# A decoder layer step on one core: weight loads, state rows and a weight split moved, and the causal term of the first head's blocks 2 to 4 added on VectorE

## What is computed

```python
proj = jnp.einsum('btd,dp->btp', xn, w_in)
gb, gc, hc, zc, q, k, v, o, zm, ig, fg = jnp.split(proj, ...)
yc, conv_new = short_conv(gc * hc, conv_buf, conv_w)      # 3 taps
y_conv = gb * yc * jax.nn.silu(zc)
# mLSTM, per head and chunk of 128 tokens
log_d = jnp.where(causal, b[:, None] - b[None, :] + ig[None, :], -jnp.inf)
m_t = jnp.maximum(b + m_prev, jnp.max(log_d, axis=-1))
d = jnp.exp(log_d - m_t[..., None]); inter = jnp.exp(b + m_prev - m_t)
s = (q @ k.T) * d
num = s @ v + inter[..., None] * (q @ c_prev)
den = s.sum(-1) + inter * (q @ n_prev)
h = num / jnp.maximum(jnp.abs(den), jnp.exp(-m_t))[..., None]
c_new = decay * c_prev + einsum(w_last, k, v)             # and n_new, m_new
y_m = rmsnorm_head(h) * gain * sigmoid(o) * silu(zm)
out = x + concat([y_conv, y_m]) @ w_out, then a last rmsnorm
```

## Time and profile before

| what | us |
|---|---|
| median of 3 runs | 1112.46 (1112.3 to 1112.65) |
| the profiled execution | 1110.13 |
| its span, first to last instruction | 1108.3 |
| PE busy, of the span | 1062.8 (96%) |
| DVE busy | 540.1 (49%) |
| ACT busy | 340.1 (31%) |
| POOL busy | 256.0 (23%) |

### The profile page before, as it was taken

How to read it: one execution, slowest core, us unless ns; L and a number is a source line. 1 busy time by engine, 2 the same in 40 slices (tenths; PEclk the granted TensorE clock), 3 DMA queues, 4 the chain that set the end, 5 groups by cost and what they waited for, 6 DMA issues and landing times. The chain is left out here.

```text
span 1108.3 us, 17992 instructions
## 1 busy us (share of the span) xinstructions
PE 1062.8 (96%) x7186; PEld 602.2 (54%) x7186; DVE 540.1 (49%) x1005; ACT 340.1 (31%) x672; POOL 256.0 (23%) x333
## 2 busy tenths in 40 slices
PE   3899999999999999999999999999999999999995
PEld 3555546565666555546665555566655555444442
DVE  5786664557553434575534344755332323433333
ACT  6546434242412232434122323341122131111111
POOL 5002303021212223212122232111211121542422
PEclk9999999999999999999999999999999999999998
DMA  9474532033200211442003114410212062265651
GB/s 248 141 159 85 135 81 49 24 105 101 89 20 19 90 49 57 119 120 89 20 18 91 49 57 138 119 32 20 94 38 90 25 218 92 102 216 209 237 200 77
DMA packets 124184, 108.74 MB, mean 98 GB/s; under 512 B 42384, under 2 KB 109092, under 8 KB 124100
## 3 DMA queue, kind: packets, MB, share of 16 engines
q1 hardware_dynamic: 81952, 65.68, 20.7%
q0 software_dynamic: 7600, 25.03, 6.2%
q10 hardware_dynamic: 34548, 16.87, 5.7%
HBM read 65.43 MB, written 33.41 MB: 89 GB/s over the span
## 5 line engine op out<-in xcount | busy, mean ns | idle before, releaser
L799 PE MATMUL bank<-xTh,Wh 128*128 128x512 f16 (+2 forms) x1304 | 421.5, 342 | 8.1 <-DVE Wl L163 4.9
L800 PE MATMUL bank<-xTl,Wh 128*128 128x512 f16 (+2 forms) x1304 | 424.4, 342 | 0.0
L801 PE MATMUL bank<-xTh,Wl 128*128 128x512 f16 (+2 forms) x1304 | 424.0, 342 | 0.0
L801 PEld LDWEIGHTS bank<-xTh,Wl 128*128 128x128 f16 x1304 | 129.2, 99 | 120.5 <-issue 0.7
L799 PEld LDWEIGHTS bank<-xTh,Wh 128*128 128x128 f16 x1304 | 129.1, 99 | 116.4 <-DVE Wl L163 5.1
L800 PEld LDWEIGHTS bank<-xTl,Wh 128*128 128x128 f16 x1304 | 129.2, 99 | 108.9 <-issue 2.6
L808 PE MATMUL bank<-Wh,xTh 128*128 128x128 f16 x544 | 92.8, 219 | 0.6 <-DVE ysum L163 0.6
L809 PE MATMUL bank<-Wl,xTh 128*128 128x128 f16 x544 | 92.8, 219 | 0.0
L810 PE MATMUL bank<-Wh,xTl 128*128 128x128 f16 x544 | 92.8, 219 | 0.0
L163 ACT ACTIVATE tz<-bank 128x512 f32<-128x512 f32 x32 | 19.1, 597 | 145.1 <-PE bank L801 144.4
L671 POOL TENSOR_TENSOR ysumst<-ysum,ysumst 128x1024 f16<-128x1024 f32 x16 | 34.1, 2128 | 103.6 <-ACT ysumst L163 103.6
(11 more groups left out here) (336 smaller groups left out, 1518.7 us busy)
## 6 DMA issues: line engine op xcount, KB each, us to landing
wst<-in_w_in ACTq DMA_DIRECT2D x29, 512.0 KB, 3.8
xs<-in_x_prompt SPq DMA_DIRECT2D x22, 512.0 KB, 4.2
y_ops<-ysumst POOLq DMA_DIRECT2D x16, 512.0 KB, 3.2
w_ops<-xs SPq DMA_DIRECT2D x16, 448.0 KB, 3.8
out<-xs POOLq DMA_DIRECT2D x11, 512.0 KB, 2.9
Wh<-y_ops SPq DMA_DIRECT2D x12, 448.0 KB, 3.6
Wl<-y_ops SPq DMA_DIRECT2D x12, 448.0 KB, 4.3
y_ops<-yst POOLq DMA_DIRECT2D x16, 256.0 KB, 3.3
```

Source lines behind the costliest of these rows:

```text
L799: mm(out, wh[:, k, :], xh, start=(k == 0), stop=False)
L800: mm(out, wh[:, k, :], xl, start=False, stop=False)
L801: last = mm(out, wl[:, k, :], xh, start=False, stop=(k == KT - 1))
```

## The change

- The three weight loads at the start of block 4 of a head are issued by ACT for the second head only; for the third and fourth head SP issues each one behind the store of the slab that had its buffer (order of buffers 1, 2, 0). ACT's wait for `wo_low` is gone. The states' load stays on ACT.
- The state rows are turned by PE in the middle of the first tile, K of block 0, instead of V's, and copied by DVE behind the first gate scan, ahead of the second weight's Wl.
- The fourth weight of the first head is split in the middle of Q instead of behind V, on ACT and on DVE.
- In blocks n = 1, 2, 3 the exponents go the other heads' way: PE makes A alone, DVE adds the mask, ACT takes `eh` from A first and then `dp`. Block n = 0 stays.

```diff
-SPLIT_AT_HALF = {Q: (4,), GC: (5,), HC: (6,), GB: (7,), ZC: (8,)}
+SPLIT_AT_HALF = {Q: (3, 4), GC: (5,), HC: (6,), GB: (7,), ZC: (8,)}
...
                 for slab in range(first_slab + 1, first_slab + 4):
                     store_slab(slab)
+                    load_w(sp, 2 + first_slab // 4, slab % STAGES)
...
                 if t == V and first and b == 0:
-                    pe.wait_ge(states_in, 16 * 2)
-                    use_t1(3)
-                    nc.tensor.transpose(T1[:, 0:STATES_IN], prow[0:STATES_IN, :], ident[0:STATES_IN, 0:STATES_IN]).then_inc(t1_full, 1)
                     columns(1, MIX, t1(g, b, "mix cols", first))
...
-                    if g:
+                    if n:
                         mm(A[:, :], selneg[:, :], m, start=True, stop=True).then_inc(a_full, 1)
                     else:
                         mm(A[:, :], selneg[:, :], m, start=True, stop=False)
                         mm(A[:, :], identb[:, :], maskb[:, :].unsqueeze(1).broadcast_to([P, CH, P]), start=False, stop=True)\
                             .then_inc(a_full, 1)
-                        pe.wait_ge(n_free, n)
                         mm(N[0][:, :], selneg[:, :], m, start=True, stop=True).then_inc(e_full, 1)
...
                         for c in range(CH):
+                            if c == CH // 2:
+                                pe.wait_ge(states_in, 16 * 2)
+                                use_t1(2)
+                                nc.tensor.transpose(T1[:, 0:STATES_IN], prow[0:STATES_IN, :], ident[0:STATES_IN, 0:STATES_IN]).then_inc(t1_full, 1)
                             if c == CH - 1:
-                                gates(x_units(0), MIX, BT, 2)
+                                gates(x_units(0), MIX, BT, 3)
...
-                    if g:
-                        act.wait_ge(arg_ready, n + 1 - NB)
+                    if n:
+                        act.wait_ge(arg_ready, n)
                     else:
-                        act.wait_ge(ym_low, n)
-                        act.wait_ge(y_sums, 4 * n)
-                        act.wait_ge(a_full, n * 3 + 1)
+                        act.wait_ge(a_full, 1)
...
-            def x_end(b, t, first):
-                if first and b == 0 and t == V:
-                    split_w(0, STAGES)
...
                     act.wait_ge(w_low, (g + 1) * NT)
-                    act.wait_ge(wo_low, 4 * g)
-                    for t in range(STAGES):
-                        load_w(act, g + 1, t)
+                    for t in range(STAGES) if g == 0 else ():
+                        load_w(act, 1, t)
                     act.wait_ge(cs_out, (g + 1) * 16)
                     load_states(act, g + 1)
...
-                        if tile < NT - 1:
+                        if STAGES < tile < NT - 1:
                             gain_w(0, tile + 1)
                         split_w(0, tile)
...
                 if t == Q:
-                    if g:
+                    if n:
                         dve.wait_ge(a_full, n * 3 + 1)
                         dve.wait_ge(y_sums, 4 * n)
                         mark(tt(chunks(dp[:, :]), chunks(A[:, :]), maskb[:, :].unsqueeze(1).broadcast_to([P, CH, P]), ALU.add)
-                             .then_inc(arg_ready, 1), arg_ready, n + 1 - NB)
+                             .then_inc(arg_ready, 1), arg_ready, n)
                         dve.wait_ge(a_free, n * 3 + 1)
...
                             gain_w(0, STAGES)
                             gain_w(0, STAGES + 1)
-                            split_w(0, STAGES)
...
             gate_scan(0, 0, MIX)
+            dve.wait_ge(t1_full, 3)
+            mark(copy(par[:, 0:STATES_IN], T1[:, 0:STATES_IN]).then_inc(t1_free, 1), t1_free, 3)
             split_w(0, 1)
             gate_abs(1, BT)
             gate_turn(0, 0, MIX)
             split_w(0, 2)
-            dve.wait_ge(t1_full, 4)
-            mark(copy(par[:, 0:STATES_IN], T1[:, 0:STATES_IN]).then_inc(t1_free, 1), t1_free, 4)
             gate_scan(1, MIX, BT)
```

More of the change, by code:

```diff
@@ L1228, in at_end @@
                     act.wait_ge(sel_ready, n + 1)
-                    if g:
-                        act.wait_ge(arg_ready, n + 1 - NB)
-                    else:
-                        act.wait_ge(ym_low, n)
-                        act.wait_ge(y_sums, 4 * n)
-                        act.wait_ge(a_full, n * 3 + 1)
-                    for out, src, kind, free, value in ((eh, A, 4, a_free, n * 3 + 1), (dp, dp, 3, dp_ready, n + 1 - NB)) if g else (
-                            (dp, A, 3, a_free, n * 3 + 1), (eh, N[0], 4, e_ready, n + 1)):
+                    if n:
+                        act.wait_ge(arg_ready, n)
+                    else:
+                        act.wait_ge(a_full, 1)
+                    for out, src, kind, free, value in ((eh, A, 4, a_free, n * 3 + 1), (dp, dp, 3, dp_ready, n)) if n else (
+                            (dp, A, 3, a_free, 1), (eh, N[0], 4, e_ready, 1)):
                         if src is N[0]:
-                            act.wait_ge(e_full, n + 1)
+                            act.wait_ge(e_full, 1)
                         for c in range(CH):
@@ L1302, in act_block @@
                     at_half(g, b, t, first)
-                    if t in (HC, GB):
-                        x_end(b, t, first)
                     evacuate(g, b, t)
-                    if t not in (HC, GB):
-                        x_end(b, t, first)
                     at_end(g, b, t, first)
@@ L1351, in _ @@
             split_w(0, 2)
-            gate_logits(1, BT, 2)
+            gate_logits(1, BT, 3)
             gate_logs(1, BT)
@@ L1637, in select @@
                 dve.wait_ge(tile_done, n * NT + 1)
-                if n <= NB:
-                    dve.wait_ge(e_ready, n)
-                else:
-                    dve.wait_ge(dp_ready, n - NB)
+                if n == 1:
+                    dve.wait_ge(e_ready, 1)
+                elif n:
+                    dve.wait_ge(dp_ready, n - 1)
                 if b == 0:
@@ L1665, in at_end @@
                         mark(tt(chunks(dp[:, :]), chunks(A[:, :]), maskb[:, :].unsqueeze(1).broadcast_to([P, CH, P]), ALU.add)
-                             .then_inc(arg_ready, 1), arg_ready, n + 1 - NB)
+                             .then_inc(arg_ready, 1), arg_ready, n)
                         dve.wait_ge(a_free, n * 3 + 1)
                     else:
-                        dve.wait_ge(e_ready, n + 1)
+                        dve.wait_ge(e_ready, 1)
                     mark(tt(eh[:, :], eh[:, :], qf[:, :], ALU.mult).then_inc(q_scaled, 1), q_scaled, n + 1)
@@ L1672, in at_end @@
                     dve.wait_ge(s_full, n * 3 + 1)
-                    if g:
-                        dve.wait_ge(dp_ready, n + 1 - NB)
+                    if n:
+                        dve.wait_ge(dp_ready, n)
                     else:
-                        dve.wait_ge(a_free, n * 3 + 1)
+                        dve.wait_ge(a_free, 1)
                     mark(tt(dp[:, :], dp[:, :], S[:, :], ALU.mult).then_inc(s_free, 1), s_free, n * 3 + 1)
@@ L1802, in dve_block @@
                         output_low(SLAB_FIRST[g, b] + (t == ZM))
-            GATE_COUNTS = [1, 2] + [t1(0, b, "gates", True) for b in range(NB - 1)]
+            GATE_COUNTS = [1, 3] + [t1(0, b, "gates", True) for b in range(NB - 1)]
             COLS_COUNTS = ([t1(0, 0, "mix cols", True)] + [t1(0, b, "cols", True) for b in range(NB - 1)] +
```

## The result

The changed kernel ran at 1102.71 us median (1102.50 to 1102.83, four runs) beside 1112.38 us for the kernel before (1110.55 to 1112.65, four runs): ratio 0.9916, 95% interval 0.9904 to 0.9927. That is 9.7 us faster. The profiled executions stand closer together than the medians: 1110.13 before and 1102.67 after, 7.46 us apart.

A forecast was written before the change was run, and what follows sets the result against it. The prediction took PE's matmuls to bound the kernel (busy 1062.8 of 1108.3 us). Its terms, 1.3 + 0.4 + 0 + 3.5 + 2.2 = 7.4 us, came off the 1112.46 us median: 1105.1 us, range 1103.0 to 1108.7.

The forecast's parts named there:

- Part 1: Blocks n = 1, 2, 3: mask on DVE removes two 512-column matmuls a block from PE, 1.3 us; bounds 0 and 1.3.
- the mask brings nothing: First head: the 1.3 us of PE time come back as waits for DVE; gain 6.1 us, 1106.4; chance 0.08.
- Part 2: First block, state rows: DVE's copy and a gap leave its chain to `sel`, 0.4 us; bounds 0.36 and 0.77.
- Part 3: First block, fourth weight split later: `qfm` wait goes, new wait of about 0.5 us at GC's start; gain 0.
- The worked-out case: First block: one half-clock stretch behind `sel` costs 1.7 us, covered by 2.3 us of PE's spare time at 75.80.
- Part 4: Block 4 of second and third head: loads on SP remove both `kf` waits, 3.5 us; bounds 2.3 and 3.5.
- Part 5: Block 4 of the first three heads: PE's waits for `cn` at ZC's end go, 2.2 us; bounds 0 and 2.2.
- The step to the median: Whole kernel: runs' median stands 2.33 us above the profiled execution, so 7.4 us was taken from 1112.46, giving 1105.1.
- the ZC waits staying: Block 4: landings of weights bind DVE's chain, so the waits remain; gain 5.2 us, 1107.3; chance 0.2.
- The first block worse than its cover: First block: second slow stretch or longer GC wait exceeds 2.3 us of spare time; gain 5.9 us, 1106.6; chance 0.12.

The follow-up runs named there:

- taken back: Changed kernel without the mask's hunks, so PE adds the causal term in the first head's blocks 2 to 4 as before: 1105.66 us, ratio 0.9945.
- its own: Kernel before with only the state rows turned in K's gap and the fourth weight split behind Q's half: 1111.36 us, ratio 0.9996.
- mask and loads: Kernel before with DVE's mask and SP's weight loads, state rows and fourth weight as before: 1105.78 us, ratio 0.9940; with the state rows too 1102.74 us, 0.9914.
- mask: Kernel before with only the causal term of the first head's blocks 2 to 4 added on DVE: 1111.38 us, ratio 0.9987.
- loads: Kernel before with only the third and fourth head's first three weight loads issued by SP: 1107.33 us, ratio 0.9958.
- SP's wait: Changed kernel, SP waiting for the fifth unit's transposed loads before loading the fourth weight: 1103.70 us, ratio 0.9931; with an earlier third `cn` update 1102.44 us, 0.9919.

## Why the prediction was right, and where it was not

The forecast of "faster" held. The range held only by the ratio, at its very end (1103.1 against 1103.0), and the median lies 0.3 us outside it. The sum of 7.4 us met the 7.46 us between the profiled executions. Part of that is luck: the early landing at the start brought 1.2 us that no part had, and what Parts 4 and 5 fell short (0.2 and 1.0) takes it back.

- **Part 1, 1.3 us**: held, 1.31 in the changed kernel, 1.31 alone, 1.27 taken back. The rival that the mask brings nothing is out. DVE's addition made no new wait of PE.
- **Part 2, 0.4 us**: held at its lower bound in the changed kernel's first trace and in its own, 0.37 and 0.36. The idle time of 0.51 us stayed with DVE. Not seen: on top of mask and loads the state rows went with 1.5 us more, the stretch at half clock behind `sel` that was then missing; and PE's win at `par` was waited out at `drl`.
- **Part 3, nothing**: held, by the trace without it. Its new wait (0.47 us for about 0.5) and the use of the cover are as told, and the load of ZC's weight was not waited for by PE. The clock went otherwise than I had said: in the first trace PE idled 0.80 us and not over 2 ahead of `sel`, and the one stretch at half clock, 45.4 to 48.8, stood ahead of `sel` as in before and not behind 52. The worked-out case, one stretch behind `sel` with its cost covered at `dpm`, came in the second trace. By the Trainium skill, "TensorE: Matmul & The Clock Gate", Part 1, idle time brings the half clock; the four traces with a second stretch behind 2.1 to 2.5 us of idle time agree with it. The waits for `kf` in the third head do so only in part: of four of 1.9 to 2.2 us, one, of 2.13, was followed by half clock.
- **Part 4, 3.5 us**: held, 1.33 + 1.98 = 3.31. What I had not seen is that the removed term was no constant: the states' issue on ACT took 3.01 and 3.64 us in one trace of before and 3.23 and 3.92 in the other.
- **Part 5, 2.2 us**: mis-sized. The three ZC waits went and gave 0.59 + 0.72 + 0.82 = 2.13, as said. But I took the lead of DVE at ZC's end as lasting, and did not follow its queue on to O, where the update stood behind a gain and a split: 0.34 + 0.24 + 0.35 = 0.93 came back. The part was worth 1.2 us, not 2.2.
- **The start, in no part**: 1.2 us. The landing of one transposed load differs by 1.5 us from execution to execution of the same kernel; the changed kernel had it both ways.
- **The step to the median.** I took the 2.33 us between before's profiled execution and its median as a constant that both kernels have. It is not. In before the time goes with the length of ACT's issue (0.5 us between its two traces) and with how much of the span is at half clock (the mean clocks); the first is gone with the change, the second can still come. No trace of before stands at its median, so the 2.33 us themselves are not explained. The first four runs of the changed kernel lie within 0.33 us and 2.4 us under the forecast; the one with a trace had an early landing and one stretch at half clock, and that the other three had the same is likely and not shown. Of the six on the other chip one took 1102.88 and five 1104.38 to 1105.98, the one with a trace with a late landing and two stretches; their median, 1105.31, is the forecast number. Over both sets the gain is 7 to 10 us.
- **The rivals**: the ZC waits staying is refuted. The first block worse than its cover (1106.6) came near in the number, 1105.93 in the changed kernel's second profile, but not by its mechanism: there the landing and the half clock in the gates cost 3.1 us ahead of `sel`, and the stretch behind it was covered. Its mechanism, half clock behind `sel` beyond the cover, stands in the traces of mask, loads, and both (6.8 us, with 1.1 us of it won back at `dpm`).

What stays open: what places the first stretch at half clock, whether the state rows' place keeps the 6.8 us stretch away in every run, what the slower, untraced runs of before lose, and whether SP's wait makes the early landing certain.

## What to carry to other kernels

When a wait goes, follow the queue that it held up to the next place where the two engines meet, with the same chain of durations; a chain that begins with the waiting engine's own output keeps its length and comes out at the next meeting. Take a difference between a profiled execution and its median for a question and not for a constant: take a second trace of the same kernel before a forecast within 3 us. And read a part's worth from its steps in the aligned traces where the runs scatter by more than the part.

## What was not expected of the hardware

- The issue of one states' load on ACT's queue behind three weights' loads took 2.72 to 3.23 us in the second head and 3.64 to 3.92 in the third (four traces), 1.45 to 2.06 in the first head (fourteen), and 0.37 us alone.
- The same transposed load landed 3.3 us after its issue in some executions and 4.8 us in others of the same kernel.
- One idle time of 2.1 to 2.5 us of PE in the first block was followed by half clock over 3.4 or 6.8 us in each of the four traces that had one there; 0.5 to 0.8 us was not, in nine. In the third head a wait of 2.13 us was followed by half clock in one trace and a wait of 2.23 us in another was not.
